# All layer norms as one routine over pairs of token tiles, interleaved with the first and last quarters of the dense feed-forward

## The reference

```python
for l in range(DEPTH):                       # two layers
    u = _ln_plain(x) * (1.0 + sc1) + sh1     # norm without weights, then modulation
    mix, st = _token_mixer(u, ...)           # conv branch and gated recurrence, ends in  merged @ w_o
    x = _ln(DN_ALPHA * x + g1 * mix, ln1_g[l], ln1_b[l])
    u2 = _ln_plain(x) * (1.0 + sc2) + sh2
    f = _swiglu(u2, w1, w3, w2) if l % 2 == 0 else _moe(u2, ...)   # layer 0 dense, layer 1 top-2 of 8 experts
    x = _ln(DN_ALPHA * x + g2 * f, ln2_g[l], ln2_b[l])
```

## Time and profile before

| | us |
|---|---|
| median of the runs (three) | 2673.8 |
| the profiled execution | 2669.52 |
| its span on the slowest core (core 3) | 2667.9 |
| spans of the other cores | 2605.8 to 2639.2 |
| mean granted clock of TensorE, core 3 | 0.867 |
| PE busy | 1913.6 (72%) |
| DVE busy | 1287.6 (48%) |
| ACT busy | 817.0 (31%) |
| POOL busy | 306.9 (12%) |

### The profile page before, as it was taken

One profiled execution on the slowest core, in us unless ns is written; L12 is line 12 of the kernel. 1 busy time (PEld: TensorE's weight loads), 2 busy tenths in 40 slices (PEclk: granted clock), 3 DMA queues, 4 the chain that ended last, 5 costly groups with the idle time before them and its releaser, 6 DMA issues.

```text
span 2667.9 us, 32710 instructions; the slowest of 8 cores (2605.8 to 2667.9 us)
## 1 busy us (share of the span) xinstructions
PE 1913.6 (72%) x11358; PEld 1062.2 (40%) x11358; DVE 1287.6 (48%) x1795; ACT 817.0 (31%) x1175; POOL 306.9 (12%) x297
## 2 busy tenths in 40 slices
PE   0588899636999814688899224588899879599920
PEld 0344445323555402344455112355445545254510
DVE  1588953563332486698824665232232222133367
ACT  0688851132111114698811221111111111111101
POOL 1000000121000131000000111300000000000034
PEclk9999999867999956899999565699899989799965
DMA  8578673505578992799886701799988999656751
GB/s 182 79 101 119 110 162 60 95 0 92 90 112 125 118 149 61 126 189 179 154 162 110 88 0 43 186 194 220 221 171 202 212 221 211 132 122 155 180 174 80
DMA packets 93867, 359.59 MB, mean 135 GB/s; under 512 B 6464, under 2 KB 6976, under 8 KB 87488
## 3 DMA queue, kind: packets, MB, share of 16 engines
q0 software_dynamic: 63568, 240.71, 56.6%
q1 hardware_dynamic: 26736, 102.93, 11.8%
q10 hardware_dynamic: 3328, 13.11, 1.2%
HBM read 539.67 MB, written 92.36 MB: 237 GB/s over the span
## 4 chain that ended last, share of the span: by engine, by line
PE 62%; DVE 15%; DMA 10%; issue 7%; ACT 4%; POOL 1%; DVEq 0%; POOLq 0%; SPq 0%; ACTq 0%
PE ps L182 62%; DMA s_big<-moe_f 4%; DVE s_mv L182 4%; DVE s_big L182 4%; DVE s_xres L182 4%; DMA s_condt<-cond 2%; ACT s_xres L182 2%; DMA s_big<-w_p 2%; DMA s_big<-xs 1%; DVE s_tw L182 1%; ACT s_big L182 1%; ACT s_tw L182 1%; DVE s_ubuf L182 1%; POOL xs L185 1%; DVE s_diag L182 1%
## 5 line engine op out<-in xcount | busy, mean ns | idle before, releaser
L182 PE MATMUL ps<-s_ubuf,s_big 128*128 128x512 bf16 (+5 forms) x6912 | 1182.0, 334 | 79.3 <-issue 46.6
L182 PEld LDWEIGHTS ps<-s_ubuf,s_big 128*128 128x128 bf16 x6912 | 670.9, 100 | 581.7 <-issue 132.2
L182 PE MATMUL ps<-s_big 128*128 128x512 bf16 (+1 forms) x2820 | 617.0, 376 | 116.3 <-DVE s_big L182 38.8
L182 DVE TENSOR_TENSOR s_big<-ps,s_big 128x1024 f32<-128x1024 f32 (+8 forms) x423 | 299.3, 711 | 779.3 <-PE ps L182 774.9
L182 PEld LDWEIGHTS ps<-s_big 128*128 128x128 bf16 x2820 | 279.3, 100 | 439.2 <-issue 166.6
L182 ACT ACTIVATE s_big<-ps 128x512 f32<-128x512 f32 (+5 forms) x322 | 154.2, 485 | 759.8 <-PE ps L182 695.3
L182 ACT ACTIVATE s_tw<-ps 128x512 f32<-128x512 f32 (+2 forms) x194 | 102.3, 547 | 405.4 <-PE ps L182 399.9
L182 ACT ACT_TABLE_LOAD x83 | 106.5, 1283 | 348.9 <-PE ps L182 151.6
L182 POOL TENSOR_TENSOR s_xres<-s_xres,s_tw 128x1024 f32<-128x1024 f32 x40 | 120.1, 3028 | 369.5 <-DVE s_xres L182 369.5
L185 POOL DMA_DIRECT2D s_big<-moe_f x72 | 52.3, 727 | 831.1 <-PE ps L182 728.5
L182 PE MATMUL ps<-s_identb,s_tw 128*128 128x128 bf16 x240 | 30.2, 307 | 158.4 <-ACT s_tw L182 156.1
(11 more groups left out here) (93 smaller groups left out, 1094.1 us busy)
## 6 DMA issues: line engine op xcount, KB each, us to landing
pc<-moe_f POOLq DMA_DIRECT2D x48, 1024.0 KB, 26.3
s_big<-pc SPq DMA_DIRECT2D x48, 1024.0 KB, 11.3
s_big<-moe_f POOLq DMA_DIRECT2D x48, 1024.0 KB, 20.0
s_big<-moe_f POOLq DMA_DIRECT2D x24, 1536.0 KB, 16.5
s_big<-w_p POOLq DMA_DIRECT2D x32, 1024.0 KB, 17.0
s_big<-w_mod POOLq DMA_DIRECT2D x24, 1024.0 KB, 17.4
s_big<-ffn_f POOLq DMA_DIRECT2D x12, 1024.0 KB, 10.6
ys<-s_tw SPq DMA_DIRECT2D x1, 10240.0 KB, 187.9
```

The lines of the kernel that those rows point to most:

```text
L182: getattr(eng, name)(*a, **kw).then_inc(sems[e], 1)
```

## The change

**One norm routine over pairs.** `moments` takes the statistics of two tiles. `affine` applies them with two fused DVE operations per tile, `(x - mean) * weight` and then `* rstd + bias` (both `scalar_tensor_tensor`); ACT computes only the square root and POOL takes no part. `plain` normalises on ACT as before; `turn_u` transposes into the fixed PSUM banks 6 and 7, and ACT alone applies the modulation. For the experts `adapt_moe` does norm and modulation with two fused DVE operations.

**One loop.** `tail` walks over five pairs. It emits for each pair: gate and residual of the two tiles, the matmuls of the next tiles (at most three are ahead, in banks 0 to 5), the finish and transposition of the pair before, and the norms of this pair. p3 of both layers and the last quarter of the dense feed-forward use it.

**The feed-forward.** The first quarter's w1 and w3 matmuls are emitted inside p3's loop (`ffn_first`): the group of tokens 0 to 511 after the fourth pair's norms, the other two around the last transposition. The w2 matmuls of the third quarter are moved to the end and accumulate in PSUM with those of the fourth (20 matmuls for each tile). The partial sum of the first two quarters is gated and added to `xres` in the second quarter.

**Broadcast rows.** `build_bc` builds all eight diagonals with one DVE operation and takes two fp32 matmuls of 512 columns.

**Precasts.** They are issued at other places: none in the first quarter, two for each f1 piece in the second and third (12), and 12 in a row at the end of the fourth; before it was one for each f1 piece (11) and eight in the fourth. In p3 of layer 1 two are left instead of seven.

The diff, cut to its core:

```diff
+        def moments(tbs, eps_col):
...
+        def rstd(m):
+            rs, mean, mk_, rk, k = m
+            dve(lambda e: e.reciprocal(out=rs[:, 2:4], in_=rs[:, 0:2]), [rk], [rk])
+        def scaled(out, src, mul, add, keys, m, outk, mulk, addk):
+            for i in range(2):
+                dve(lambda e, i=i: e.scalar_tensor_tensor(out=out[i], in0=src[i], scalar=mean[i], in1=mul[i], op0=ALU.subtract, op1=ALU.mult),
+                    [keys[i], mk_[i], mulk[i]], [outk[i]])
+            rstd(m)
+            for i in range(2):
+                dve(lambda e, i=i: e.scalar_tensor_tensor(out=add[i][0], in0=out[i], scalar=rs[:, 2 + i:3 + i], in1=add[i][1],
+                                                          op0=ALU.mult, op1=ALU.add), [outk[i], rk, addk[i]], [add[i][2]])
...
+        def turn_u(l, p, shc, scc):
+            for i in range(2):
+                for c in range(NCH):
+                    pe(lambda e, c=c, i=i: e.transpose(out=psb[:, 6 + i, c * 128:(c + 1) * 128], in_=xnbf[:, i * D + c * 128:i * D + (c + 1) * 128],
+                                                       identity=identb[:]), [('xnbf', i), 'identb'], pk(6 + i))
+            for c in range(NCH):
+                act(lambda e, c=c, s1=s1, s2=s2: e.activation(out=ubuf[:, c, p * 256:(p + 1) * 256].rearrange("p (a b) -> p a b", a=2),
+                                                              in_=psb[:, 6:8, c * 128:(c + 1) * 128], func=AF.Identity, scale=s1, bias=s2),
+                    pk(6, 2) + [('modT', l)], keys)
+        def build_bc(dst, keys, l, chunk0, slot, b=None):
+            dve(lambda e: e.tensor_tensor(out=dg, in0=mk(identf[:, 0:1], 0, [[0, NCH], [1, 128]]), in1=mk(modT[:, 0:1], l * 96 + chunk0 * 2 + slot, [[2, NCH], [0, 128]]),
+                                          op=ALU.mult), ['identf', ('modT', l)], ['tmA'])
+            for h in range(2):
+                pe(lambda e, h=h: e.matmul(ps[:, b + h, :], lhsT=onesf[:], rhs=tmA[:, h * 512:(h + 1) * 512], start=True, stop=True),
+                   ['onesf', 'tmA'], pk(b + h))
...
+        def tail(mm, resid, norm, turn, mid=None, late=None):
+            def fill(n):
+                while done[0] < min(n, NTB):
+                    mm(done[0], 2 * (done[0] % 3))
+                    done[0] += 1
+            fill(3)
+            for p in range(5):
+                for tb in (2 * p, 2 * p + 1):
+                    resid(tb, 2 * (tb % 3))
+                fill(2 * p + 5)
+                if fin:
+                    fin()
+                if p:
+                    turn(p - 1)
+                fin = norm([2 * p, 2 * p + 1])
+                if p == 3 and mid:
+                    pst['reserved'] = {0, 1, 4, 5}
+                    mid()
+                    pst['reserved'] = set()
+            fin()
+            if late:
+                late(1)
+            turn(4)
+            if late:
+                late(2)
...
+                        ffn1(q, i, slot, skey, range(3))
+                if q < 2:
+                    part = ffn_w2(l, q)
...
+                            add_gated(f_acc[:, tb, :], [('facc', tb)], tb, gt[tb // 8], GK[tb // 8])
+            load_lnbc(l, 2)
+            build_bc(gbcB, ['gbcB', ('facc', 9)], l, 40, 1)
+            mod_job(l + 1, 3)
+            for i in range(0, 4, 2):
+                slot, skey = ring_next(('f1', l, 0, 3, i))
+                ffn1(3, i, slot, skey, range(3))
+            parts = [ffn_w2(l, 2), ffn_w2(l, 3, hold=1)]
+            precast(12)
...
+            tail(lambda tb, b: ffn2(tb, b, parts), lambda tb, b: add_gated(psrc(b), pk(b, 2), tb, gbcB if tb > 7 else gbc, 'gbcB' if tb > 7 else 'gbc', False),
+                 norm, lambda p: turn_u(l + 1, p, 0, 8))
...
-                for j in range(3):
-                    build_u(l, j, 0, 8, lambda tb: ('x', tb))
+                if l == 0:
+                    for p in range(5):
+                        plain([2 * p, 2 * p + 1])()
+                        turn_u(l, p, 0, 8)
...
+                    for s in range(2):
+                        build_bc(scb[s], [SCK[s]] + ([('xnbf', 1)] if s else []), l, 32, s, 6)
+                        build_bc(shb[s], [SHK[s]], l, 24, s, 6)
+                    tail(mm, resid, norm_m, turn_moe)
...
+                    tail(mm, resid, norm_d, lambda p: turn_u(l, p, 24, 32), lambda: ffn_first(l, 0), lambda j: ffn_first(l, j))
```

336 lines of the change are left out of this document (159 added, 177 removed).

## The result

The changed kernel takes 2559.0 us (median of three runs, 2557.6 to 2563.1) beside 2674.3 for the kernel before in the same session: a ratio of 0.9576, 95% interval 0.9536 to 0.9617. The forecast was 2550, the range 2500 to 2605. The profiled execution took 2563.1 us, with a span of 2561.4 on core 3; the other cores end between 2495.4 and 2516.6. The mean clock is 0.890 to 0.894 on all eight.

What follows compares the result with a forecast made beforehand. Norm stretches were taken as a DVE, ACT, POOL chain leaving PE partly idle. Gains 24 + 39 + 60 + 14.5 less 8.6, 4 and 5 gave 120 off 2669.5: 2550 us, range 2500 to 2605.

Steps and rivals of the forecast that it cites:

- The pair of 22 to 24 us: New pair loop: a middle pair takes 22 to 24 us, 23 assumed, because ACT modulates the previous pair before the root.
- The start: Before p1 of layer 0: ACT alone does all modulations, 9.7 us per pair, p1 begins at 108.8, loss 8.6 us.
- p3 of layer 0 with the first quarter: Stage from p3 of layer 0 to the first w2: 197.6 us before, 174 after, gain 24.
- Rival (c): DVE's fused operations on `xres` and `tw` cost 2.6 us each, 140 us more on DVE's chain: 2690; chance 0.04.
- Rival (b): PE stays at half clock in short pieces between norms, `w_o` of two tiles taking 14 us: 2625 us; chance 0.05.
- The weights term: Precasts bunched at new places delay weight loads: 4 us charged in the quarters, 5 for p1 of layer 1.
- its own mark: Sign of failure: PE waits for `s_big<-ffn_f` or `s_big<-w_p` for more than 25 us in sum.
- The queue gets 4 us late by the fourth quarter: Feed-forward's second and third quarter: six precasts each, at 8.5 us, delay weights; 4 us charged, 20 late at 10 us each.
- the p1 piece behind them lands 3 to 25 us late: Twelve end precasts and stores need 117 to 135 us beside a 120 us loop, delaying p1's weights; 5 us charged.
- Rival (a): Precasts take the norms' place: weight waits at each quarter's f1 and w2 and p1 of layer 1, 40 to 60 us; chance 0.12.
- p3 of layer 1: From p3 of layer 1 to the routing: 210 us before, 149 after, with 28 for six spread rows; gain 60.
- The last norm: Final norm: a pair takes 13.4 us, five take 67, the store behind stays as it is; gain 14.5 us.

Runs made afterwards that it cites:

- the first two experiments: Changed kernel with ten tail precasts moved to `w_o` of layer 0: 2579.8 us; with precasts spread over `w_o`, first quarter and f1 pieces: 2521.2 and 2532.7 us.

## Why the prediction held, and where it did not

**Right, and shown.** The direction and the main cause: norms that leave GpSimd, and lose ACT's turn. The old affine norm, put back alone, costs 97 us of the 106.5 by the spans, the old rows 32 by the stages, the missing interleaving 5; the parts do not add up, since the wait for weights hides some of each and the new place of the precasts makes the first dearer. The pair of 22 to 24 us, held by ACT's modulations ahead of the root: 23.1 and 22.1 measured in p3, and 16 once the root stands ahead. The start: +8.1 against +8.6, undone by splitting ACT's work. p3 of layer 0 with the first quarter: -22.0 against -24. Rival (c), slow fused operations, is out: 2.47 us for two, 1.23 to 1.28 each. Rival (b), the half clock, is out as priced: while the 32 `w_o` matmuls of a pair ran, the granted clock was 0.70 and 0.81, and they took 9.93 and 8.64 us, neither the 7.0 of full speed nor the 14 of half.

**The weights term was mis-sized.** The prediction charged 4 us for the queue in the quarters and 5 for p1 of layer 1. By its own mark, more than 25 us of waits for `s_big<-ffn_f` or `s_big<-w_p`, it was wrong: 49.5, less the 12.7 that went, is 37, so 28 more than the 9 charged. Two steps failed. "The queue gets 4 us late by the fourth quarter" took the precasts at 8.5 us beside an even flow; they came in twos ahead of every f1 piece, the DMA share was 0.92 from 676 to 911, and the waits there were 18.7 us, 15 more than charged. And "the p1 piece behind them lands 3 to 25 us late" took 117 to 135 us of DMA beside a loop of 120; the loop was about as long as forecast (117.5 us), but the last store needed 19 us, held GpSimd's next issue to 1024, and the piece then took 36.9 us: a wait of 30.8, 13 more than charged. Rival (a) was thus in part true, its mechanism shown by the first two experiments, and at 28 us smaller than its 40 to 60.

**The terms that made it up.** p3 of layer 1 gained 72.5 instead of 60: the six rows took 22 us in place of 28, since a 512-column fp32 product is 0.98 us, near the lower bound of 1, the first pair 16.5 in place of 18, and a later pair 21.2 in place of 22.1. The last norm gained 20 instead of 14.5: a pair is 12.9 instead of 13.4, and what stands behind the last pair 3 us instead of 6. In the tail of the feed-forward, the stage without its 18.7 us of waits gained 42 where 39 were counted. The errors of +28 on one side and -12.5, -5.5 and -3 on the other, with some 6 us of small ones, give the 13.5 us between the forecast sum of 120 and the measured 106.5. So the mechanism was right, but that the time came within 0.4% of the forecast was in part luck: a loss that was sized too small and gains that were sized too small cancelled.

**Argued in the prediction, now corrected.** The price of GpSimd's addition was taken as DVE's multiplication of 2.08 us in place of 1.23. The runs show it to be wider: in the last stage the DVE operations with two SBUF inputs that meet an addition are held (3.36 and 3.17 us, of which the earlier trace rows had one at 3.35), while one alone takes 1.2 to 1.3. The mean of 2.08 mixes the two: in p3 of layer 0 of the kernel before, four multiplications together took 8.92 and 8.93 us, and the last two 2.36. And an addition queued behind DMA issues waits for what they wait for. That the interleaving with the first quarter is a gain by itself was part of the description; it is 5 us.

**Left open.** Why the experts' stage differs by up to 12 us between kernels with the same code there was not tried. Three parts of the change were not undone by themselves: the loop over pairs, the third quarter's w2 kept in PSUM, and the experts' fused modulation. What each is worth is not shown.
